# Matmul operands moved 64 bytes down against the weight slots in SBUF, and fp32 products of constants put ahead of the 512-column units, in a three-block transformer kernel

## The chip, the cores and the metric

The program runs on one core of one Trainium2 chip. The metric is the device time of one execution in microseconds, lower is better; the time quoted is the median of the runs of a kernel. The profile is of one execution, taken by the hardware profiler.

## What is computed

256 tokens of width 1024 pass through a chain of blocks, all in fp32. First come two layers of a block with modulation, for a latent sequence x and a context sequence ctx of 256 tokens each:

```
for layer in range(2):
    h  = h  + 0.5 * g1  * swiglu(prenorm(h),  ffn1)      # both sequences: 512 tokens
    hc = hc + 0.5 * cg1 * swiglu(prenorm(hc), ffn1)
    mix_l, mix_c = (even_mixer, odd_mixer)[layer](prenorm(h), prenorm(hc))
    h  = h + gm * (mix_l @ mix_w_out)                     # the context too in layer 0
    h  = h + 0.5 * g2 * swiglu(prenorm(h), ffn2)          # the context too in layer 0
return rmsnorm(h)
swiglu(h) = (silu(h @ w_g) * (h @ w_u)) @ w_out           # 1024 -> 2816 -> 1024
```

The even mixer is a Fourier mix with gated linear attention, the odd one a short convolution with differential attention. Behind them, for the 256 tokens of x alone, come a retention block, a feed-forward block c0, a dilated attention block, and a feed-forward block c1, each with a residual and a layer norm. The weights, some 400 MB, are read once.

## The kernel before

**Products.** Each fp32 product is made of three fp32r products (`product3`, L271): weights and activations are split into a high and a low part, and hi x hi, hi x lo and lo x hi are summed in PSUM. The split weights lie in three slots of 8192 bytes per partition each (`w_hi`, `w_lo`), written by ScalarE (line L105 in the profile) and VectorE (L109) from four slots `w_raw` that SyncE's queue loads. In the profile all these products are "L98 PE MATMUL bank<-x_hi,w_hi" and its like. Normally a 128x128 block of the weights is the stationary operand and the activations x, hid, even, odd, rt or at move past it: 512 columns wide in the stages of both sequences, 256 in the stages of one. In some projections the roles are exchanged (`project_rows`, L316): the activations are stationary and 256 columns of weights move ("bank<-w_hi,x_hi"). Below, a wide product is one of 512 columns, a narrow one is one of 256.

**Order.** The order of all engines is the program's. A feed-forward stage (`pe_ffn`, L832; called a0, b0, a1, b1, c0, c1) goes over its 22 blocks of 128 hidden columns two at a time: j = 0, 2, ... 10, then the products with w_out for these (4 chunks of two units), then j = 12 ... 20, then w_out again. One j is two units of 48 products. After each j, and after each chunk of w_out, `between` may put in a few fp32 products for the modulation: four-row-group products with the tile `sums`, or with `fold`. a0, b0 and a1 have 512 columns, b1, c0 and c1 have 256.

**Places.** All tiles have fixed places. `hT`, `ident`, `ones`, `cs`, `diag` and other small tiles come first, then `w_raw`, `w_hi`, `w_lo`, then coef (64 bytes), rs (96), lam (32) and a pad of 64 bytes, then a work area in which `place` puts the activations at XN, MID or TEMPS. XN and MID are multiples of 256 bytes, and the slots are multiples of 8192, so in the kernel before the work area begins at the weights' position modulo 256. Three constants shift single tiles: the narrow input x2 is placed at XN + BACK, BACK = -64; the hidden tile of the narrow stages (`hidden`, L819), and the tiles of the odd mixer and of retention, at MID + FORTH, FORTH = 192, which is -64 modulo 256. The wide x, the wide hidden tile, the tile even_hi and even_lo, and the tiles of the dilated attention but for at_hi have no shift.

**The extra product.** `pe_realign` (L648) issues one fp32 product of 256 columns of constants into a spare PSUM bank that nobody reads. It is called ahead of j = 4 in b1, c0 and c1 (`if j == 4 and n == T`), ahead of the output product of retention, and once in the dilated attention.

Of the kernel before, what the change touches and what calls it, by code (L numbers as in the profile page):

```python
# [7 lines left out]
P = 128  # L8
F32 = mybir.dt.float32
F32R = mybir.dt.float32r  # L10
# [5 lines left out]
KC = D // P  # L16
T = 256
# [32 lines left out]


XN, MID, TEMPS, WORK = 0, 32768, 90496, 106880
PAD, BACK, FORTH = 64, -64, 192
UNIT = 2048
NRAW, NSPLIT = 4, 3

# [267 lines left out]
def pe_pair(e, u, x, n, names, taken):  # L324

    for q in range(2):
        bank = e.bank(names[q], *taken[q])
        project(e, u, q * P, x, n, bank).then_inc(e.k.product, names[q])
    u.last = names[1]
# [315 lines left out]
        e.matmul(bank[:, 0:P], k.ident[:, :], k.ones[:, :], True, True)  # L645


def pe_realign(e):  # L648

    k = e.k  # L650
    bank = e.bank("spare", None, None)
    del e.used[k.bank_at["spare"]]
    for _ in range(1):
        e.matmul(bank[:, 0:T], k.ident[:, :], k.small_t[:, 0:T], True, True)


def pe_rms_rows(e, nid, n, taken):
# [166 lines left out]
def in_name(f, j, base, q):  # L824
    return (f, "in", j, base, q)


def out_name(f, half, m):
    return (f, "out", half, m)


def pe_ffn(e, f, w_in, w_out, x, n, between, gate):  # L832
    k, e.ada_owed = e.k, True
    for half, (j0, jn) in enumerate(HALVES):
        for j in range(j0, j0 + jn, 2):
            names = [in_name(f, j, base, q) for base in range(2) for q in range(2)]
            taken = [(k.scalar, (f, "silu", j, q)) for q in range(2)] + [(k.vector, (f, "gated", j, q)) for q in range(2)]
            if j == 0 and f == "a0":
                pass
            elif j == 0:  # L840
                us = [take(e, (f, "in", j, base), w_in, 0, KC, base * FFN, 256) for base in range(2)]
                project_first(e, us, x, n, names, taken)
            else:
                if j == 4 and n == T:
                    pe_realign(e)
                for base in range(2):
                    u = take(e, (f, "in", j, base), w_in, 0, KC, base * FFN + j * P, 256)
                    pe_pair(e, u, x, n, names[2 * base:2 * base + 2], taken[2 * base:2 * base + 2])
            between(e)
        if half == 0:  # L850
            gate(e)
        hid, hk = hidden(k, (f, half), n), jn // 2
        for c in range(KC // 2):
            names = [out_name(f, half, 2 * c + q) for q in range(2)]
            banks = [e.bank(names[q], k.vector, ("h", f, half, 2 * c + q)) for q in range(2)]
            for part in range(2):
                u = take(e, (f, "out", half, c, part), w_out, j0 + part * hk, hk, c * 256, 256)
                for q in range(2):
                    project(e, u, q * P, hid, n, banks[q], range(part * hk, part * hk + hk), part * hk, part == 0,
                            part == 1).then_inc(k.product, (names[q], part))  # L860
                u.last = (names[1], part)
            between(e)
# [872 lines left out]
class Odd:  # L1735
    NS = 3

    def __init__(self, k):
        at = MID + FORTH
        self.q = k.place("df_q", at, [P, 6, T])  # L1740
        self.k = k.place("df_k", at + 6144, [P, 6, 2 * T])
        self.v = k.place("df_v", at + 18432, [P, 4, 768])
        self.z3 = k.place("df_z", at + 8192, [P, 3, 2, T])
        self.cs = k.place("df_cs", at + 36864, [P, 2, T])
        self.rot = k.place("df_rot", at + 38912, [P, P])
        self.raw = k.place("df_raw", at + 39424, [P, 4, T])
        self.rt = k.place("df_rt", at + 43520, [P, 2, T])
        self.y = k.place("df_y", at + 45568, [P, 2, T])

        self.sc = k.place("df_sc", at + 47616, [P, 12, 8])  # L1750

        self.norm = k.place("df_norm", at + 48000, [P, 3, 12])
        self.sq = k.place("df_sq", at + 48192, [P, P])
        self.e = k.place("df_e", TEMPS, [P, self.NS, 2, 2 * T])

        self.aT = k.place("df_aT", at + 30720, [P, self.NS, 4, P])
        self.o = k.place("df_o", at + 39424, [P, 12, P])

        self.out = Operand(("mix", 1), k.place("odd_hi", at + FORTH + 48704, [P, KC, T], F32R), k.place("odd_lo", at, [P, KC, T], F32R))

        self.dst = [self.q[:, m, :] for m in range(6)] + [self.k[:, m, 0:T] for m in range(6)]

# [1340 lines left out]
def build(nc, io):  # L3103
    with ExitStack() as ctx:
        def sb(name, shape, dt=F32):
            return ctx.enter_context(nc.sbuf_tensor(name, shape, dt))

        def sem(name):
            return ctx.enter_context(nc.semaphore(name))

        k = Kernel()
        k.nc, k.io, k.new_sem = nc, io, sem
        k.hT, k.small_t, k.ident = sb("hT", [P, KC, 2 * T]), sb("small", [P, SMALL_N]), sb("ident", [P, P])
        k.ones, k.eps, k.one = sb("ones", [P, P]), sb("eps", [P, 2]), sb("one", [P, 1])
        k.cs, k.fold, k.mod_t = sb("cs", [P, KC, 38]), sb("fold", [P, 8]), sb("mod", [P, 2 * MODS * KC, 2])
        k.sel = sb("sel", [P, 39])
        k.mean = k.cs[:, :, :].rearrange("p k c -> p (k c)")[:, 0:P]
        k.gate, k.rs2, k.diag = sb("gate", [P, KC, 2]), sb("rs2", [P, 24]), sb("diag", [P, 4, P])
        k.raw = sb("w_raw", [P, NRAW, UNIT])
        k.whi, k.wlo = sb("w_hi", [P, NSPLIT, UNIT], F32R), sb("w_lo", [P, NSPLIT, UNIT], F32R)  # L3120
        k.coef, k.rs, k.lam = sb("coef", [P, KC, 2]), sb("rs", [P, 24]), sb("lam", [P, 8])
        sb("pad", [P, PAD // 4])
        k.work = (nc.sbuf_base + 31) // 32 * 32
        assert k.work + WORK <= nc.sbuf_top
        k.placed = {}
        k.psum = [ctx.enter_context(nc.psum_tensor(f"bank{i}", [P, 512], F32)) for i in range(8)]
        k.acc = k.place("acc", TEMPS, [P, 2 * T])
        k.spread = k.acc[:, T:2 * T]
        k.sq = k.place("sq", TEMPS + 2048, [P, 2, 2 * T])
        k.mean_row = k.sq[:, 0, T:2 * T]  # L3130
        k.tmp = k.place("tmp", TEMPS + 6144, [P, 2, 2 * T])
        k.sg = k.sq2 = k.place("sg", TEMPS + 10240, [P, 2, 2 * T])
        k.ada_rows = k.place("ada_rows", TEMPS + 14336, [P, 2, 256])
        k.sums = [k.place(f"sums{i}", MID + 49152 + 4096 * i, [P, 2, 512]) for i in range(2)]
        k.x2 = Operand(None, k.place("x2_hi", XN + BACK, [P, KC, T], F32R), k.place("x2_lo", XN + BACK + 8192, [P, KC, T], F32R))
        k.x = Operand(None, k.place("x_hi", XN, [P, KC, 2 * T], F32R), k.place("x_lo", XN + 16384, [P, KC, 2 * T], F32R))

        k.product = Signal("product", sem("s_product"))
        k.scalar, k.w_hi = Signal("scalar", sem("s_scalar")), Signal("w_hi", sem("s_w_hi"))
        k.vector, k.w_lo = Signal("vector", sem("s_vector")), Signal("w_lo", sem("s_w_lo"))  # L3140
        k.pooled = Signal("pooled", sem("s_pooled"))
        k.raw_in = [Signal(f"raw{i}", sem(f"s_raw{i}"), 16) for i in range(NRAW)]
        k.bias_in = [Signal(f"bias{i}", sem(f"s_bias{i}"), 16) for i in range(4)]
        k.loads, k.bank_at = {}, {}
        k.stream, k.split, k.units, k.others = [], [], {}, []
        counting = [True]

        def after(ahead, others):

            if counting[0]:  # L3150
                k.others.append((len(k.stream) + ahead, others))
        k.after = after

        for program in (pe_program, act_program, dve_program, pool_program, sp_program):
            program(Engine(k))
        counting[0] = False
        for signal in (k.product, k.scalar, k.w_hi, k.vector, k.w_lo, k.pooled, *k.raw_in, *k.bias_in, *k.loads.values()):
            signal.value = 0

        block = ctx.enter_context(nc.Block())  # L3160

        @block.sync
        def _(e):
            sp_program(Engine(k, e))

        @block.tensor
        def _(e):
            pe_program(Engine(k, e))

        @block.scalar  # L3170
        def _(e):
            act_program(Engine(k, e))

        @block.vector
        def _(e):
            dve_program(Engine(k, e))

        @block.gpsimd
        def _(e):
            pool_program(Engine(k, e))  # L3180
# [125 lines left out]
```

How the kernel before makes its waits and increments, by code:

```python
    def then_inc(self, signal, *events):  # L69
        signal.value += signal.step
# [18 lines left out]
    def wait_ge(self, signal, event):  # L89
        if self.eng is None:
            return
        n = signal.at[event]
        if n > self.waited.get(signal.name, 0):
            self.eng.wait_ge(signal.sem, n)
            self.waited[signal.name] = n
# [41 lines left out]
    def bank(self, name, signal, event, hold=False, of=None):  # L137
        if of is not None:
            b = of[self.turns.get(of, 0) % len(of)]
            self.turns[of] = self.turns.get(of, 0) + 1
        else:
            while self.turn in self.holds:
                self.turn = (self.turn + 1) % 8
            b = self.turn
            self.turn = (b + 1) % 8
        if hold:
            self.holds.add(b)
        if b in self.used:
            self.wait_ge(*self.used[b])
        self.used[b] = (signal, event)
        self.k.bank_at[name] = b
        return self.k.psum[b]
# [45 lines left out]
def take(e, name, w, k0, kn, c0, cn, split=True, book=False, summed=False):  # L201
# [11 lines left out]
            u.turn = len(k.split)  # L213
            u.hi_flat, u.lo_flat = k.whi[:, u.turn % NSPLIT, 0:kn * cn], k.wlo[:, u.turn % NSPLIT, 0:kn * cn]
            u.hi, u.lo = (t.rearrange("p (k c) -> p k c", k=kn) for t in (u.hi_flat, u.lo_flat))
            k.split.append(u)
        k.stream.append(u)
        k.units[name] = u
    u = k.units[name]
    if book:
        return u
    if split:
        e.wait_ge(k.w_hi, u.index)
        e.wait_ge(k.w_lo, u.index)
    else:
        e.wait_ge(k.raw_in[u.slot], u.index)
```

## Time and profile before

| | |
|---|---|
| time, median of 3 runs | 2644.91 us (2644.59 to 2647.29) |
| time of the profiled execution | 2645.05 us |
| span from first to last instruction | 2643.3 us |
| mean granted TensorE clock | 0.993 of full speed |
| TensorE busy | 2583.0 us of the span (98%) |
| VectorE busy | 1483.6 us (56%) |
| ScalarE busy | 1040.9 us (39%) |

An instruction's duration in the profile runs from its issue to its modelled end, and matmuls overlap in it: two consecutive products of 389 ns can start 227 ns apart. The rate at which TensorE works is therefore read from the starts, or from a piece of the chain of waits: its length divided by the number of matmuls in it. An fp32 product appears as two MATMUL records.

### The profile page before, as it was taken

To read this page: it belongs to the slowest core of one execution; us is meant where nothing else is said; L and a number is where in the kernel's file an instruction comes from. 1 tells how busy PE (TensorE), PEld (TensorE's weight loads), DVE (VectorE), ACT (ScalarE), POOL (GpSimd) and SP (SyncE) were. 2 spreads that over 40 slices of the span, in tenths; PEclk is the share of its full clock that TensorE was granted. 3 is DMA by queue.
4 is the path that set the end of the run, shared out by engine and by line. 5 is a ranking of instruction groups with operands and counts; after the bars stand their busy time and mean duration, and the time that the engine had idled before them with its cause. 6 is when DMAs were issued, how large, how long until landed. Compare 5 with 4: busy or idle time off the path is not lost.

```text
span 2643.3 us, 40453 instructions
## 1 busy us (share of the span) xinstructions
PE 2583.0 (98%) x17454; PEld 2278.0 (86%) x17454; DVE 1483.6 (56%) x1985; ACT 1040.9 (39%) x1402; POOL 199.2 (8%) x192
## 2 busy tenths in 40 slices
PE   6999999999999999999999999999999999999998
PEld 4788888877888888888878899999999999988998
DVE  5666654746556546553345565566555554565655
ACT  3322223534222224222233554453754454554544
POOL 0000000211000000000011000010020020144001
PEclk9999999999999999999999999999999999999999
DMA  7544455214444444443153165565446566763462
GB/s 259 177 159 149 154 166 164 64 62 149 133 149 146 141 159 152 146 156 120 60 171 126 49 195 188 182 211 169 146 152 196 182 194 187 218 148 119 149 207 91
DMA packets 376080, 405.98 MB, mean 154 GB/s; under 512 B 7264, under 2 KB 352176, under 8 KB 375904
## 3 DMA queue, kind: packets, MB, share of 16 engines
q1 hardware_dynamic: 375904, 403.40, 47.9%
q8 instruction: 138, 2.26, 0.4%
q14 instruction: 38, 0.31, 0.0%
HBM read 402.25 MB, written 1.12 MB: 153 GB/s over the span
## 4 chain that ended last, share of the span: by engine, by line
PE 90%; DVE 4%; issue 3%; ACT 2%; POOL 1%; DMA 1%; SPq 0%; DVEq 0%; POOLq 0%; ACTq 0%
PE bank L98 89%; DVE w_lo L109 1%; PE bank L101 1%; ACT w_hi L105 1%; POOL acc L109 1%; DVE tmp L117 0%; DMA ident<-in_ident 0%; DVE df_sc L126 0%; ACT df_e L106 0%; ACT x_hi L105 0%; DVE hT L117 0%; DMA w_raw<-in_ada_w 0%; ACT at_pT L105 0%; ACT at_e L106 0%; ACT L105 0%
## 5 line engine op out<-in xcount | busy, mean ns | idle before, releaser
L109 DVE TENSOR_TENSOR w_lo<-w_raw,w_hi 128x2048 fp32r<-128x2048 f32 (+2 forms) x331 | 698.4, 2114 | 740.4 <-ACT w_hi L105 739.8
L98 PE MATMUL bank<-x_hi,w_hi 128*128 128x256 f32 (+1 forms) x3000 | 976.8, 326 | 5.0 <-DVE w_lo L109 2.0
L98 PE MATMUL bank<-x_hi,w_lo 128*128 128x256 f32 (+1 forms) x3000 | 966.5, 322 | 0.0
L98 PE MATMUL bank<-x_lo,w_hi 128*128 128x256 f32 (+1 forms) x3000 | 961.6, 322 | 0.0
L105 ACT ACTIVATE w_hi<-w_raw 128x2048 fp32r<-128x2048 f32 (+2 forms) x331 | 578.9, 1753 | 377.3 <-PE bank L98 221.2
L98 PEld LDWEIGHTS bank<-x_hi,w_hi 128*128 128x128 f32 x3000 | 564.7, 188 | 66.0 <-issue 15.1
L98 PEld LDWEIGHTS bank<-x_hi,w_lo 128*128 128x128 f32 x3000 | 564.7, 188 | 47.6
L98 PEld LDWEIGHTS bank<-x_lo,w_hi 128*128 128x128 f32 x3000 | 562.3, 188 | 47.3 <-issue 0.7
L98 PE MATMUL bank<-hid_hi,w_hi 128*128 128x512 f32 (+1 forms) x1056 | 353.0, 334 | 0.0
L98 PE MATMUL bank<-hid_hi,w_lo 128*128 128x512 f32 (+1 forms) x1056 | 351.4, 333 | 0.0
L98 PE MATMUL bank<-hid_lo,w_hi 128*128 128x512 f32 (+1 forms) x1056 | 351.2, 333 | 0.0
L105 ACT ACTIVATE hid_hi<-tmp 128x512 fp32r<-128x512 f32 (+1 forms) x132 | 69.3, 525 | 415.5 <-DVE tmp L109 415.5
L98 PEld LDWEIGHTS bank<-hid_hi,w_hi 128*128 128x128 f32 x1056 | 198.2, 188 | 24.6 <-issue 4.1
L98 PEld LDWEIGHTS bank<-hid_hi,w_lo 128*128 128x128 f32 x1056 | 198.2, 188 | 20.8
L98 PEld LDWEIGHTS bank<-hid_lo,w_hi 128*128 128x128 f32 x1056 | 198.3, 188 | 20.2
L117 DVE SCALAR_TENSOR_TENSOR sums<-w_raw,cs,sums 128x512 f32<-128x512 f32 x308 | 207.7, 746 | 0.0
L109 POOL TENSOR_TENSOR acc<-acc,sq 128x256 f32<-128x256 f32 (+1 forms) x60 | 60.9, 1015 | 1475.1 <-ACT sq L105 1474.0
L98 PE MATMUL bank<-w_hi,x_hi 128*128 128x256 f32 x544 | 156.7, 288 | 0.0
L98 PE MATMUL bank<-w_lo,x_hi 128*128 128x256 f32 x544 | 152.7, 281 | 0.0
L98 PE MATMUL bank<-w_hi,x_lo 128*128 128x256 f32 x544 | 152.6, 281 | 0.0
L105 ACT ACTIVATE sg<-bank 128x512 f32<-128x512 f32 (+1 forms) x132 | 63.5, 485 | 214.3 <-PE bank L98 214.3
L109 DVE TENSOR_TENSOR hid_lo<-tmp,hid_hi 128x512 fp32r<-128x512 f32 (+1 forms) x132 | 73.8, 559 | 78.0 <-ACT hid_hi L105 78.0
(278 smaller groups left out, 2333.5 us busy)
## 6 DMA issues: line engine op xcount, KB each, us to landing
w_raw<-in_ffn_w_in SPq DMA_DIRECT2D x88, 1024.0 KB, 6.1
w_raw<-in_ada_w SPq DMA_DIRECT2D x72, 1024.0 KB, 8.0
w_raw<-in_ffn_w_up SPq DMA_DIRECT2D x44, 1024.0 KB, 5.2
w_raw<-in_attn_w_in SPq DMA_DIRECT2D x36, 1024.0 KB, 5.2
w_raw<-in_ffn_w_out SPq DMA_DIRECT2D x32, 768.0 KB, 4.7
w_raw<-in_ret_w_in SPq DMA_DIRECT2D x24, 1024.0 KB, 5.4
w_raw<-in_ffn_w_out SPq DMA_DIRECT2D x32, 640.0 KB, 4.3
w_raw<-in_odd_w_in SPq DMA_DIRECT2D x12, 1024.0 KB, 5.4
```

What stands on the lines that cost most here:

```text
L98: return Issued(self.eng and self.eng.matmul(out, lhsT, rhs, start=start, stop=stop, skip_group_check=loose))
L101: return Issued(self.eng and self.eng.transpose(out, in_, self.k.ident[:, :]))
L105: return Issued(self.eng and self.eng.activation(out, in_, func, bias=bias, scale=scale))
L109: return Issued(self.eng and self.eng.tensor_tensor(out, a, b, op))
L117: return Issued(self.eng and self.eng.scalar_tensor_tensor(out, a, s, b, op0, op1))
```

## The change

It has three parts.

1. coef, rs and lam, 192 bytes together, move from behind the weight slots to ahead of them, and the pad behind the slots grows from 64 to 192 bytes. The work area now begins 192 bytes, that is -64 modulo 256, after the weights' position. BACK and FORTH become 0, so x2, the narrow hidden tile and the tiles of the odd mixer and of retention keep their -64 against the weights; at_hi too. The wide x, the wide hidden tile, even_hi and even_lo, the wide and narrow use of x in both mixers, and at_lo go from 0 to -64.
2. `pe_realign` takes a number of 128-column blocks and a number of repeats; the moving operand is now the identity tile, repeated, where it was the tile small.
3. In a0 and b0 it is called ahead of each j from 4 to 20, with the lengths of the table REALIGN, and in a1 once, ahead of j = 4, with 4 blocks. The calls in the narrow stages keep their place and length.

```diff
-PAD, BACK, FORTH = 64, -64, 192
+PAD, BACK, FORTH = 64, 0, 0
...
-def pe_realign(e):
+REALIGN = {4: (2, 1), 6: (1, 1), 8: (4, 1), 10: (2, 2), 12: (1, 2), 14: (4, 2), 16: (2, 3), 18: (1, 3), 20: (2, 1)}
+
+
+def pe_realign(e, blocks=2, times=1):
 
     k = e.k
     bank = e.bank("spare", None, None)
     del e.used[k.bank_at["spare"]]
-    for _ in range(1):
-        e.matmul(bank[:, 0:T], k.ident[:, :], k.small_t[:, 0:T], True, True)
+    wide = k.ident[:, :].rearrange("p (o n) -> p o n", o=1).broadcast_to([P, blocks, P])
+    for _ in range(times):
+        e.matmul(bank[:, 0:blocks * P].rearrange("p (o n) -> p o n", o=blocks), k.ident[:, :], wide, True, True)
...
-                if j == 4 and n == T:
+                if n == T and j == 4:
                     pe_realign(e)
+                if n == 2 * T and f != "a1" and j in REALIGN:
+                    pe_realign(e, *REALIGN[j])
+                if f == "a1" and j == 4:
+                    pe_realign(e, 4, 1)
...
-        self.out = Operand(("mix", 1), k.place("odd_hi", at + FORTH + 48704, [P, KC, T], F32R), k.place("odd_lo", at, [P, KC, T], F32R))
+        self.out = Operand(("mix", 1), k.place("odd_hi", at + 48640 + 256, [P, KC, T], F32R), k.place("odd_lo", at, [P, KC, T], F32R))
...
+        k.coef, k.rs, k.lam = sb("coef", [P, KC, 2]), sb("rs", [P, 24]), sb("lam", [P, 8])
         k.raw = sb("w_raw", [P, NRAW, UNIT])
         k.whi, k.wlo = sb("w_hi", [P, NSPLIT, UNIT], F32R), sb("w_lo", [P, NSPLIT, UNIT], F32R)
-        k.coef, k.rs, k.lam = sb("coef", [P, KC, 2]), sb("rs", [P, 24]), sb("lam", [P, 8])
-        sb("pad", [P, PAD // 4])
+        sb("pad", [P, 3 * PAD // 4])
```

## Rows read from the trace of the kernel before

**Rows 1.** The page: busy time, share and instructions; granted clock in 40 slices.

```profile
PE 2583.0 (98%) x17454; PEld 2278.0 (86%) x17454; DVE 1483.6 (56%) x1985; ACT 1040.9 (39%) x1402; POOL 199.2 (8%) x192
PEclk9999999999999999999999999999999999999999
```

**Rows 2.** The chain that ended last: shares of the span by engine.

```profile
PE 90%; DVE 4%; issue 3%; ACT 2%; POOL 1%; DMA 1%; SPq 0%; DVEq 0%; POOLq 0%; ACTq 0%
```

**Rows 3.** Waits of PE: total us, times, longest.

```profile
PE bank L98 <- DVE w_lo L109: 3.0, 4, 1.0
```

**Rows 4.** Busy time by stretch, all engines: a0, then b0.

```profile
60.00:450.00 390.00, 389.12 (x1819) 314.55 (x1819) 237.66 (x321) 109.30 (x120) 8.48 (x7) 1.00 0.49 161
620.00:1010.00 390.00, 390.00 (x1875) 316.14 (x1878) 219.43 (x299) 108.80 (x120) 9.95 (x8) 1.00 0.45 150
```

**Rows 5.** Groups of PE by form, whole span: count, busy us, mean ns, idle before.

```profile
L98 PE MATMUL bank<-x_hi,w_hi 128*128 128x256 f32 x1792 | 501.4, 280 | 3.6 <-DVE w_lo L109 2.0 <-DVE x_lo L117 1.1 <-ACT x_hi L105 0.2
...
L98 PE MATMUL bank<-x_hi,w_hi 128*128 128x512 f32 x1208 | 475.4, 394 | 1.4 <-ACT sg L105 0.8 <-DVE x_lo L117 0.5
...
L98 PE MATMUL bank<-hid_hi,w_hi 128*128 128x512 f32 x528 | 207.3, 393 | 0.0
...
L98 PE MATMUL bank<-even_hi,w_hi 128*128 128x512 f32 x64 | 25.4, 397 | 2.9 <-ACT even_hi L105 2.9
```

**Rows 6.** Chain pieces: start us, length us, what; wide products of a0, then a1.

```profile
109.89 16.32 PE bank L98 x72
...
1214.91 155.27 PE bank L98 x685
```

**Rows 7.** Chain pieces: narrow products on x, not shifted (even mixer), then shifted (b1).

```profile
456.92 10.08 PE bank L98 x84
...
1599.99 140.08 PE bank L98 x1236
...
1576.00 4.59 PE bank L98 x39
```

**Rows 8.** Timeline of PE around the call of pe_realign in b1: start, us.

```profile
1586.56 0.28 PE L98 MATMUL bank<-x_lo,w_hi 128*128 128x256 f32 x1
1586.68 0.28 PE L98 MATMUL bank<-x_hi,w_lo 128*128 128x256 f32 x1
1586.80 0.59 PE L98 MATMUL bank<-small,ident 128*128 128x256 f32 x2
1587.04 0.47 PE L98 MATMUL bank<-x_hi,w_hi 128*128 128x256 f32 x1
1587.35 0.28 PE L98 MATMUL bank<-x_lo,w_hi 128*128 128x256 f32 x1
1587.47 0.28 PE L98 MATMUL bank<-x_hi,w_lo 128*128 128x256 f32 x1
1587.59 0.28 PE L98 MATMUL bank<-x_hi,w_hi 128*128 128x256 f32 x1
```

**Rows 9.** Timeline of PE: other fp32 products ahead of shifted narrow ones.

```profile
1574.80 0.51 PE L98 MATMUL bank<-fold,ada_rows 128*128 128x8 f32 x4
1575.16 0.36 PE L98 MATMUL bank<-x_hi,w_hi 128*128 128x256 f32 x1
1575.36 0.28 PE L98 MATMUL bank<-x_lo,w_hi 128*128 128x256 f32 x1
1575.48 0.28 PE L98 MATMUL bank<-x_hi,w_lo 128*128 128x256 f32 x1
1575.60 0.28 PE L98 MATMUL bank<-x_hi,w_hi 128*128 128x256 f32 x1
1575.72 0.28 PE L98 MATMUL bank<-x_lo,w_hi 128*128 128x256 f32 x1
...
1841.74 2.73 PE L98 MATMUL bank<-rt_v,rt_S 128*128 128x512 f32 x6
1843.91 0.68 PE L98 MATMUL bank<-w_hi,x_hi 128*128 128x256 f32 x1
1844.43 0.28 PE L98 MATMUL bank<-w_lo,x_hi 128*128 128x256 f32 x1
```

**Rows 10.** Timeline of PE after `sums` in a0: start, us.

```profile
105.16 0.64 PE L98 MATMUL bank<-sums,sel 128*32 128x256 f32 x8
105.73 0.50 PE L98 MATMUL bank<-x_hi,w_hi 128*128 128x512 f32 x1
106.07 0.39 PE L98 MATMUL bank<-x_lo,w_hi 128*128 128x512 f32 x1
106.30 0.39 PE L98 MATMUL bank<-x_hi,w_lo 128*128 128x512 f32 x1
106.53 0.40 PE L98 MATMUL bank<-x_hi,w_hi 128*128 128x512 f32 x1
106.77 0.39 PE L98 MATMUL bank<-x_lo,w_hi 128*128 128x512 f32 x1
107.00 0.40 PE L98 MATMUL bank<-x_hi,w_lo 128*128 128x512 f32 x1
107.23 0.39 PE L98 MATMUL bank<-x_hi,w_hi 128*128 128x512 f32 x1
107.46 0.39 PE L98 MATMUL bank<-x_lo,w_hi 128*128 128x512 f32 x1
107.69 0.39 PE L98 MATMUL bank<-x_hi,w_lo 128*128 128x512 f32 x1
```

**Rows 11.** Groups of PE by form: even mixer (440 to 545 us), odd mixer (1375 to 1556 us).

```profile
L98 PE MATMUL bank<-w_hi,x_hi 128*128 128x256 f32 x128 | 36.5, 285 | 0.0
...
L98 PE MATMUL bank<-w_hi,x_hi 128*128 128x256 f32 x96 | 28.8, 300 | 0.0
L98 PE MATMUL bank<-x_hi,w_hi 128*128 128x256 f32 x96 | 28.0, 293 | 1.3 <-DVE x_lo L117 1.1
```

## The prediction

> **What bounds the kernel.** Read the page first: TensorE is busy 98% of the span at full clock, VectorE 56% [rows 1]. The chain of waits says the same: 90% of it is TensorE's own work [rows 2]. The waits of PE for split weights come to 3.0 us in all [rows 3]. By stretch, a0 and b0 keep PE busy without a gap, with VectorE at 61% and 56% of the time and the DMA engines under half [rows 4]. So nothing is late behind TensorE in the wide stages, and each nanosecond taken from a matmul there, or added to it, is a nanosecond of the time.
>
> Next, how fast the matmuls follow each other. There are 1208 + 528 + 64 = 1800 wide products, each of three matmuls: 5400 [rows 5]. In steady work they start 16.32 / 72 = 226.7 ns apart in a0 and 155.27 / 685 = 226.7 ns apart in a1 [rows 6]. 512 columns at the granted 2.4 GHz are 213.3 ns, so each carries 13.3 ns, or 32 cycles, of something else.
>
> The narrow ones tell what part of it depends on place. 256 columns are 106.7 ns. With x at the weights' position modulo 256 (even mixer) they start 10.08 / 84 = 120.0 ns apart: again 13.3 ns over. With operands at -64 (b1) they do so at 140.08 / 1236 = 113.3 ns, 6.7 over, and in the same stage a little earlier at 4.59 / 39 = 117.7, 11 over [rows 7]. So at -64 there are two steady rates, and one is kept until something breaks the stream. The call of pe_realign leads from the slow to the fast one: 0.12 us between starts before it, 0.11 after [rows 8]. Other fp32 products ahead of narrow ones end differently: after `fold` the starts lie 0.12 us apart, after a 512-column product 0.11 [rows 9].
>
> **The move, wide products.** No row shows a wide fp32r product at -64. The bounds: nothing gained, 226.7; or all of the 13.3 ns gone, 213.3, which would be 5400 x 13.3 = 72 us. I take the narrow rows as the model, because the excess at 0 is the same 13.3 ns for both widths. That speaks for a cost paid once per matmul, where its stream and the load of the next block meet, and not one per column. Then a wide product at -64 costs 220.0 in the good state, saving 6.7 ns, or 224.4 (213.3 + 11) in the poor one, saving 2.2.
>
> Which state? The narrow stages settle once and run on for over a thousand matmuls. a0 and b0 are cut again and again by `sums` and `fold`: after `sums` eight starts at 0 lie 0.23 to 0.24 us apart before the stream settles [rows 10]. At -64 each such break draws a state anew. `fold` gave the poor one in the narrow case, the extra product of 256 columns and one of 512 the good one [rows 8, 9]. I take three quarters good, one quarter poor: 0.75 x 6.7 + 0.25 x 2.2 = 5.6 ns, and 5400 x 5.6 = 30.0 us. All good gives 36.0, all poor 11.9.
>
> **The move, narrow products.** 3 x 128 in the even mixer and 3 x (96 + 96) in the odd one go from 0 to -64 [rows 11]: 960 matmuls, cut often by other products, half in each state: 960 x 4.4 = 4.2 us; between 2.1 and 6.4. at_lo joins at_hi at -64 (192 matmuls, under 1 us), taken as nothing. The fp32 products of the mixers get other places too; bounded by the same 6.7 ns on a few hundred, and of unknown sign, they are left at nothing.
>
> A rule stands against all this. The Trainium skill, page "SBUF — State Buffer", section "Who interferes with whom", says that PE waits for no one and that its two read ports, for the moving operand and for the weight load, are independent. By it a place would not matter; this trace disagrees, with 120.0 against 113.3 ns for the same matmul. The Trainium skill's page "TensorE: Matmul & The Clock Gate", section "Back-to-back issue gap", gives N/2.4 + 2.5 ns, 215.8 at 512 columns; by it the wide part would save 5400 x 10.9 = 59 us, an estimate; the narrow rows do not come down to its 109.2 ns here.
>
> **The extra products.** Without the call in b1, the next matmul on x_hi,w_hi would have started at 1586.80 and the one three places on 0.35 us later; the latter started at 1587.59, 0.79 us later: 0.44 us for 256 columns [rows 8]. Three 512-column products: the second matmul behind them starts 2.69 us after their start, and 0.11 of it is that matmul's own distance, which leaves 0.86 us each [rows 9]. So the cost goes by columns. The table has 2 + 1 + 4 + 4 + 2 + 8 + 6 + 3 + 2 = 32 blocks of 128, 16 times the 256-column product: 16 x 0.44 = 7.04 us, in each of a0 and b0, and 0.88 in a1: 15.0 us in all. Nothing covers it, since PE waits for nothing there [rows 4]; nearly all of them stand where `sums` or `fold` has broken the stream already, so no second settling is added. The spare bank turns the order of banks by one, but in these stages seven or eight banks serve five allocations per j of 22 us, so the next user finds its bank read long ago.
>
> VectorE and ScalarE see their tiles moved against each other by multiples of 64 bytes; taken as nothing, and hidden by PE in any case [rows 4]. Where PE gets 2.5% faster VectorE goes from 61% to 63% of a0.
>
> **The sum.** 2645.05 - 30.0 - 4.2 + 15.0 = 2625.8 us. The profiled execution lies 0.1 us above the median of 2644.91, so 2625.7.
>
> **The rivals.**
>
> *A. The wide products do go faster, in both states mixed (the forecast).* From 11.9 + 2.1 saved up to 36.0 + 6.4 saved; with at least half in the good state (5400 x 4.4 = 24.0) it is 2614 to 2637. Chance 0.53.
>
> *B. The wide ones find only the poor state.* The 128-column and odd lengths of the table are untried before fp32r products at -64. 2645.0 - 11.9 - 2.1 + 15.0 = 2646.0. Chance 0.10.
>
> *C. The wide ones don't change (the move does nothing).* Weight loads are busy for 81% of a0 [rows 4], so a wide product leaves them slack, and its excess may come from elsewhere, with the equal 13.3 ns a chance. Then 2645.0 - 4.2 + 15.0 = 2655.8, slower than before. It decides from the point where the mean saving of a wide matmul is under (15.0 - 4.2) / 5400 = 2.0 ns. Against it: equal excess at both widths. Chance 0.17. If the place does nothing for the narrow ones either, 2645.0 + 15.0 = 2660.0; the three narrow rates of this trace speak against it [rows 7]: 0.04. This last case is the one that the Trainium skill's SBUF page stands for.
>
> *D. The narrow stages lose their good state.* pe_realign reads the identity for both operands now. If that ends in the poor state, some 1390 matmuls of each of b1, c0 and c1 (all behind j = 2) go from 113.3 to 117.7: 3 x 1390 x 4.4 = 18.4 us, and the time would be 2625.7 + 18.4 = 2644.1. Against it: the same length and the same stationary tile. Chance 0.09.
>
> *E. The wide ones get slower.* After `sums` six starts take 107.46 - 106.07 = 1.39 us, 231.7 ns each [rows 10]; if -64 made that lasting, 5400 x 5.0 = 27 us more: 2645.0 + 27 - 4.2 + 15.0 = 2682.8. Chance 0.07.
>
> **Numbers.** What a measurement can tell from no change is 0.2%, 5.3 us: 2639.6 to 2650.2. Faster: A, and a part of D: 0.57. Same: most of B and half of D: 0.12. Slower: C, E and the rest: 0.31. The range goes from 2614 (all wide and narrow products in the good state give 2645.0 - 36.0 - 6.4 + 15.0 = 2617.6, and 3 us for fp32 products that gain too) to 2660, which takes in B, C and D and leaves E; A alone is 2614 to 2637.
>
> **What would show it.** In the profile after, a piece of the chain inside a0 or a1, its length over its count: 220 in the good state, 224.4 in the poor, 226.7 if C holds. The mean duration of the wide groups, 389 to 394 ns now [rows 5], follows by the same difference. The stretch of a1 with no `sums` behind 1215 us shows one state alone. In b1, c0 and c1 the starts after the extra product should stay at 113.3; else it is D. The products of ident with ident should take about 0.21 us per 128 columns. The forecast is wrong if the wide stream has a steady state of its own that the narrow one doesn't have: its weight load has slack, the narrow one's has little.

## The result, and the profile after

The changed kernel takes 2693.49 us (median of 4 runs, 2689.58 to 2694.50) against 2644.76 for the kernel before, 48.7 us or 1.8% more. The comparison on record puts the ratio at 1.0165, with a 95% interval of 1.0142 to 1.0187; it is not the quotient of the two medians, but both lie well clear of no change. The ratios further down are of the same kind. I had forecast 2625.7, faster, in a range that ended at 2660. The change loses 49 us where I expected it to gain 19.

The page of the changed kernel, the lines that answer to [rows 1] and [rows 2]:

```profile
PE 2630.3 (98%) x17520; PEld 2290.0 (85%) x17520; DVE 1483.1 (55%) x1985; ACT 1041.2 (39%) x1402; POOL 199.9 (7%) x192
PEclk9999999999999999999999999999999999999999
...
PE 89%; DVE 4%; issue 3%; ACT 3%; DMA 1%; POOL 1%; SPq 0%; DVEq 0%; POOLq 0%; ACTq 0%
```

TensorE is still all of it, at the same clock, and busy 47 us longer. VectorE and ScalarE do what they did. 66 MATMUL records are new: 33 fp32 products of two records each, 16 in a0, 16 in b0 and 1 in a1.

Groups of PE by form, whole span, for [rows 5] (count, busy us, mean ns, idle before):

```profile
L98 PE MATMUL bank<-x_hi,w_hi 128*128 128x256 f32 x1792 | 503.5, 281 | 3.9 <-DVE w_lo L109 2.0 <-DVE x_lo L117 1.1 <-ACT x_hi L105 0.3
...
L98 PE MATMUL bank<-x_hi,w_hi 128*128 128x512 f32 x1208 | 485.1, 402 | 1.1 <-ACT sg L105 0.6 <-DVE x_lo L117 0.5
...
L98 PE MATMUL bank<-hid_hi,w_hi 128*128 128x512 f32 x528 | 210.5, 399 | 0.0
```

The narrow group is as it was, 281 ns for 280. The wide ones went from 394 to 402 and from 393 to 399 (the groups of x and of hid). Pieces of the chain of waits give the distance of the starts, for [rows 6] and [rows 7]: wide in a1, narrow in the even mixer, narrow in b1. In the even mixer it is the weights that move and x that is stationary.

```profile
1261.91 103.13 PE bank L98 x442
...
475.45 9.66 PE bank L98 x82
...
1644.93 135.09 PE bank L98 x1192
```

103.13 / 442 = 233.3 ns for the wide product, where it was 226.7. 9.66 / 82 = 117.8 in the even mixer, where it was 120.0. 135.09 / 1192 = 113.3 in b1, as before. So a wide matmul pays 20.0 ns beyond its 213.3, three times the 6.7 ns of the good narrow state, and neither the 6.7 nor the 11 of the forecast. The timeline of PE around an added product in a1 (for [rows 8] and [rows 10]):

```profile
1093.40 0.39 PE L98 MATMUL bank<-x_hi,w_lo 128*128 128x512 f32 x1
1093.63 1.02 PE L98 MATMUL bank<-ident 128*128 128x512 f32 x2
1094.09 0.79 PE L98 MATMUL bank<-x_hi,w_hi 128*128 128x512 f32 x1
1094.72 0.39 PE L98 MATMUL bank<-x_lo,w_hi 128*128 128x512 f32 x1
1094.95 0.40 PE L98 MATMUL bank<-x_hi,w_lo 128*128 128x512 f32 x1
1095.19 0.39 PE L98 MATMUL bank<-x_hi,w_hi 128*128 128x512 f32 x1
1095.42 0.40 PE L98 MATMUL bank<-x_lo,w_hi 128*128 128x512 f32 x1
1095.65 0.39 PE L98 MATMUL bank<-x_hi,w_lo 128*128 128x512 f32 x1
```

Behind it the starts lie 0.23 to 0.24 us apart, as they do without it.

Where the time went, from the starts of the first product of each stage in each profile (us; the last four columns are experiments of the next section):

```
                       before  after  move_only  products_only  wide_plus64  no_products
a0 (from its first)     379.8  397.3    388.9        389.9         384.8        381.7
even mixer              226.8  228.5    228.4        226.8         226.4        226.5
b0                      368.2  385.1    378.1        375.2         371.4        368.2
norm ahead of a1          6.9    8.5      6.9          6.9           6.9          6.9
a1                      364.0  375.0    374.1        364.9         367.3        364.0
odd mixer               189.2  186.6    187.6        187.7         189.1        189.9
b1                      187.3  187.7    187.3        187.1         187.1        194.1
retention               210.5  210.0    210.2        210.5         210.8        210.2
c0                      190.2  189.7    189.5        189.3         189.3        195.7
dilated, projections    136.3  140.9    138.5        141.1         136.1        138.4
dilated, the rest       159.5  158.9    159.1        158.2         158.8        159.0
c1                      195.7  195.7    196.2        202.4         196.0        201.5
```

45.4 of the 49.4 us of span are in a0, b0 and a1. The other large line is the dilated attention's projections, 4.6 us.

Differences of a microsecond or two in this table need the granted clock beside them. The first 8 us from 28 us on, of the kernel before, products_only and no_products (the clock is the third number from the end):

```profile
28.00:36.00 8.00, 8.00 (x53) 5.33 (x46) 3.51 (x11) 1.72 (x5) 0.00 (x0) 0.86 1.09 348
```

```profile
28.00:36.00 8.00, 8.00 (x47) 4.73 (x40) 2.49 (x9) 1.29 (x3) 0.00 (x0) 0.68 1.09 348
```

```profile
28.00:36.00 8.00, 6.99 (x36) 3.99 (x29) 2.55 (x6) 1.70 (x5) 0.00 (x0) 0.57 1.09 348
```

TensorE stands at 1.2 GHz for part of these 8 us, in some executions for longer. A share of 0.68 for 0.86 takes 0.18 of 8 us of full speed away, 1.4 us; 0.57 takes 2.3 us. The 1.6 us of the norm ahead of a1 are of the same kind, since the granted clock there was 0.80 in the changed kernel and 1.00 in the kernel before. In b0 and a1 the clock was full in the kernel before, in products_only and in the changed kernel.

### The profile page after: what moved, and what is told of

The parts are those of the page before. It is cut to its first block, busy times and chain, and to the rows that moved or that the text cites. A ratio compares the mean times of both kernels' runs of the same rounds, so it can differ in the third digit from the quotient of the medians.

```text
span 2692.7 us, 40582 instructions
## 1 busy us (share of the span) xinstructions
PE 2630.3 (98%) x17520; PEld 2290.0 (85%) x17520; DVE 1483.1 (55%) x1985; ACT 1041.2 (39%) x1402; POOL 199.9 (7%) x192
## 4 chain that ended last, share of the span: by engine, by line
PE 89%; DVE 4%; issue 3%; ACT 3%; DMA 1%; POOL 1%; SPq 0%; DVEq 0%; POOLq 0%; ACTq 0%
PE bank L98 88%; DVE w_lo L109 1%; ACT w_hi L105 1%; PE bank L101 1%; POOL acc L109 1%; DMA w_raw<-in_ada_w 0%; DVE hT L117 0%; DVE tmp L117 0%; DVE df_sc L126 0%; DMA ident<-in_ident 0%; DVE sums L117 0%; ACT df_e L106 0%; ACT x_hi L105 0%; ACT at_pT L105 0%; ACT at_e L106 0%
## 5 line engine op out<-in xcount | busy, mean ns | idle before, releaser
L98 PE MATMUL bank<-x_hi,w_hi 128*128 128x256 f32 (+1 forms) x3000 | 988.5, 330 | 5.0 <-DVE w_lo L109 2.0
```

The source lines that it names most:

```text
L98: return Issued(self.eng and self.eng.matmul(out, lhsT, rhs, start=start, stop=stop, skip_group_check=loose))
```

## The experiments

**Apart: the move alone, the products alone.** The first leaves the calls in the wide stages out of the changed kernel (everything else as there):

```diff
-                if n == 2 * T and f != "a1" and j in REALIGN:
-                    pe_realign(e, *REALIGN[j])
-                if f == "a1" and j == 4:
-                    pe_realign(e, 4, 1)
```

> The changed kernel without the products ahead of the wide units (they stay in the narrow stages). Theory 1, a wide matmul at -64 starts every 233.3 ns whatever stands ahead of it: 5400 x 6.67 = 36.0 us more, 4 less in the mixers, some 5 more in the dilated attention: about 2679 to 2683, and every long wide stretch of the chain at 233.3 ns. Theory 2, the added products themselves put the wide stream into a slow state: wide stretches at 220 or 226.7 ns and 2618 to 2645.

The second is the kernel before with the new `pe_realign` (its body is that of the change) and its calls, and nothing moved:

```diff
...
-                if j == 4 and n == T:
+                if n == T and j == 4:
                     pe_realign(e)
+                if n == 2 * T and f != "a1" and j in REALIGN:
+                    pe_realign(e, *REALIGN[j])
+                if f == "a1" and j == 4:
+                    pe_realign(e, 4, 1)
```

> The kernel before with the added products and nothing moved. Theory 1: the wide stretches stay at 226.7 ns and the time rises by the products alone, 15.0 us: 2660. Theory 2, that the products slow the wide stream: wide stretches over 226.7 ns and up to 2695. If the products ahead of j find cover: under 2652.

move_only takes 2676.41 us, 1.0114 times the kernel before (1.0092 to 1.0136). products_only takes 2668.50, 1.0078 times (1.0053 to 1.0102). The first is 3 us under the range of its first theory, the second 8 us over its 2660: in the stage table c1 is 6.7 us longer and the dilated projections are 4.8 us longer, two narrow stages that no added product of the wide ones touches. A wide piece of the chain in a1, of move_only and then of products_only:

```profile
1244.99 95.20 PE bank L98 x408
```

```profile
1235.82 94.29 PE bank L98 x416
```

95.20 / 408 = 233.3 ns with the move and no added product; 94.29 / 416 = 226.7 with the products and no move. So the wide rate follows the place, and the products do nothing to it at either place. Theory 1 holds in both. In the stage table the move costs 9.1, 9.9 and 10.1 us in a0, b0 and a1, near the 1584 x 6.67 = 10.6 of each stage, and the products cost 10.1, 7.0 and 0.9.

The 7.0 and 0.9 are the forecast's terms to the tenth. In a0 there are 3 us more, and about half of them is a wait that I had ruled out. The timeline of PE in the changed kernel's a0:

```profile
270.43 0.64 PE L98 MATMUL bank<-sums,sel 128*32 128x256 f32 x8
272.42 1.99 PE L98 MATMUL bank<-ident 128*128 128x512 f32 x4 [1.35 <-ACT ada_rows L105]
273.84 0.82 PE L98 MATMUL bank<-x_hi,w_hi 128*128 128x512 f32 x1
```

The spare bank fell on the one that `sums` had just filled and ScalarE had yet to read. `pe_sums` holds that bank only until its own products are issued, not until they are read, so the next allocation may get it. In products_only the same wait is 1.67 us:

```profile
268.94 1.98 PE L98 MATMUL bank<-ident 128*128 128x512 f32 x4 [1.67 <-ACT ada_rows L105]
```

The rest is the clock at the start of a0, shown above: 7.0 + 1.7 + 1.4 = 10.1 us. In the changed kernel, where the clock of those 8 us was 0.85, nearly that of the kernel before, a0 adds up without it: 9.1 for the move, 7.0 for the products and 1.35 of waiting make the 17.5 measured. In no_products, whose a0 has the same instructions as the kernel before, the clock alone gives 1.9 us more.

**A list of places.** A kernel of its own runs 72 fp32r matmuls of the kernel's pattern (hi x hi, hi x lo, lo x hi, with blocks changing) for each place of the moving operand against the stationary one. It computes nothing of the reference.

```diff
+SECTIONS = [(n, p, 0, 128) for n in (512, 256) for p in (*range(0, 256, 32), 16, 48, 208, 240)]
+SECTIONS += [(n, p, s, 128) for n in (512, 256) for p, s in ((64, 64), (0, 64), (128, 128), (64, 128), (0, 128))]
+SECTIONS += [(512, p, 0, m) for m in (64, 32) for p in (0, 192)]
...
+            for n, p, s, m in SECTIONS:
+                e.matmul(psum[7][:, 0:T], ident[:, :], hT[:, 0, 0:T], start=True, stop=True)
...
+                        e.matmul(bank[0:m, 0:n], hi, x0, start=kk == 0, stop=False)
+                        e.matmul(bank[0:m, 0:n], lo, x0, start=False, stop=False)
+                        e.matmul(bank[0:m, 0:n], hi, x1, start=False, stop=kk == KC - 1)
```

> Not the computation: 72 fp32r matmuls for each of a list of places, with the moving operand 0 to 240 bytes above the stationary one modulo 256, 512 and 256 columns wide, some with the stationary operand moved as well, some with a stationary block of 64 or 32 columns. Theory 1, the excess depends on the place of one operand against the other: 226.7 ns at 0 and 233.3 at 192 for 512 columns, 120.0 and 113.3 (or 117.7) for 256, the same at (64, 64) and (128, 128) as at (0, 0), and less excess with a narrower stationary block. Some other place may give 220 or less for 512 columns. Theory 2, the excess depends on the absolute place: (64, 64) differs from (0, 0). Theory 3, it comes from something else in the kernel, such as the other engines' accesses: all places alike here.

Mean distance of the starts behind the 20th, in ns:

```
bytes of the moving operand against the stationary one, modulo 256
            0      16     32     48     64     96     128    160    192    208    224    240
512 wide  226.7  231.6  233.3  233.3  228.9  233.3  232.6  234.3  233.4  234.7  233.3  236.6
256 wide  120.0  118.7  116.7  118.4  117.8  119.9  118.6  118.7  113.3  119.1  118.4  117.1
both operands up by 64: 226.7 and 120.0; by 128: 226.7 and 120.0
only the stationary one up by 64 (that is 192): 233.4 and 113.3
the stationary one up by 128, the moving one by 64 (192 again): 233.4 and 117.8
512 wide, stationary block of 64 columns: 229.8 at 0, 232.7 at 192; of 32: 231.7 and 231.6
```

This gives the kernel's rates again in a program with no other engine at work: 226.7 and 120.0 at 0, 233.4 and 113.3 at 192, which is -64. For the wide stream it is the place of one operand against the other that counts: the two entries at 0 with both moved, and the two further ones at 192, give the same as before. The narrow one has 113.3 and 117.8 at 192, the two steady rates of [rows 7]. In the mixers' exchanged projections the weights move, so x at -64 is place 64 of this list, with its 117.8: the 117.8 of the even mixer. The two widths don't follow each other. The best wide place is the narrow stream's worst of these, and from 160 to 240, where the narrow one is no worse than 119.1, the wide one pays 233.3 to 236.6. My forecast had them parallel. A narrower block doesn't take the excess away: with 32 columns it is 18 ns at both places tried.

**Finer, and one thing changed at a time.**

```diff
+SECTIONS = [(512, p, 0, 128) for p in (0, 4, 8, 12, 20, 24, 236, 244, 248, 252, 196, 188)]
...
+SECTIONS += [(512, k, 0, 128) for k in ("line", "column", "xlo192", "xlo64", "wlo64", "wlo192", "fp32")]
+SECTIONS += [(n, p, 0, 128) for n in (384, 128) for p in (0, 192)]
+SECTIONS += [(256, k, 0, 128) for k in ("line", "column", "xlo0", "wlo64")]
...
+                        if p == "column":
+                            x0, x1 = (xs[home][:, a:a + 1].broadcast_to([P, n]) for a in (at0, at1))
```

> Not the computation: again 72 fp32r matmuls for each of a list of cases. Finer places around 0 for 512 columns and around 192 for 256. Theory 1, that the two streams meet in lines of 64 bytes: 4 to 12 bytes beside the good place give nearly the same rate, within 3 ns. Theory 2, the good places are sharp: already 4 bytes beside them it is 230 ns and more, 117 and more. Then one thing changed each: the moving operand 16 columns read again and again (line) or one column (column), the low activations or low weights at another place, plain fp32, 384 and 128 columns. If the excess is made where the moving stream crosses SBUF, line and column take it away (216 ns or less for 512 columns); if it is made behind the array, they leave it at 227. Plain fp32 should show about 216 ns between records, as the product of constants does in the kernel before.

At 4 bytes off the best place the wide rate is 237.1 ns, at 8 it is 233.3, at 12 it is 228.9: Theory 1, lines of 64 bytes, falls. With the low activations, or the low weights, alone moved off 0 it is 228.9 to 232.2. "line" (the same 16 columns again and again) gave 242.0, so a short stretch is no better. "column" (one column, 512 times) gave 217.8, which leaves 4.4 ns of the 13.3. The groups of PE in the stretch of "column" (L106 to L108 are the three matmuls):

```profile
L106 PE MATMUL bank<-x_p,w_hi 128*128 128x512 f32 x18 | 6.9, 382 | 0.0
L108 PE MATMUL bank<-x_p,w_hi 128*128 128x512 f32 x18 | 6.8, 378 | 0.0
L107 PE MATMUL bank<-x_p,w_lo 128*128 128x512 f32 x17 | 6.5, 381 | 0.0
```

Their 378 to 382 ns stand against 389 for the ordinary operand at 0. So what the moving operand reads has a part in the excess; more is not shown, since "line" went the other way and a narrow stream at 192 gained only 1.5 ns by reading one column (111.8 for 113.3). Plain fp32 was a miss: I expected some 216 ns between records and got 429.2, since the 216 of the kernel before belong to products of 256 columns. An fp32 product of 512 columns thus takes 858.4 ns, only 5 more than four times 213.3, where an ordinary fp32r matmul carries 13.3 or more by itself.

384 columns cost 173.3 ns at 0 and 176.7 at 192, against 160 for the columns themselves. Set beside the other widths this is the most useful pair of the list:

```
excess over the columns' own time, ns     256 wide   384 wide   512 wide
moving operand at 0                         13.3       13.3       13.3
at 192 (-64); 256 in its good state          6.7       16.7       20.0
```

At 0 the excess is one cost per matmul, whatever the width. At 192 it grows with the width, and the narrow stream's gain has turned into a loss already at 384 columns. (128 columns took 111.7 ns at both places, over twice their 53.3, and say nothing on it.)

**All 64 places.**

```diff
+SECTIONS = [(n, p, 0, 128) for n in (512, 256) for p in range(0, 256, 4)]
```

> Not the computation: 72 fp32r matmuls at every place of the moving operand in steps of 4 bytes, 0 to 252 above the stationary one, for 512 and for 256 columns. Theory 1, that places are sharp and irregular: most of the 64 wide places give 228 to 240 ns, 0 gives 226.7 and is the best or among the best few; most narrow ones give 117 to 125 and only a few 113.3. If a wide place under 225 ns exists, the wide stages of the kernel can gain by it. Theory 2, a smooth dependence: neighbours within 1 ns of each other.

The best wide place is 0, with 226.7 ns; then 60 (227.8), 28 and 108 (227.8), 64 and others (228.9). The worst are 68, 116, 132, 196 and 244 with 240.0. The first and last matmul of four stretches, at 0, 4, 64 and 192 (33, 31, 32 and 32 matmuls; start us, duration us):

```profile
32.75 0.39 PE L85 MATMUL bank<-x_p,w_lo 128*128 128x512 f32 x1
...
40.00 0.39 PE L84 MATMUL bank<-x_p,w_hi 128*128 128x512 f32 x1
...
50.82 0.40 PE L86 MATMUL bank<-x_p,w_hi 128*128 128x512 f32 x1
...
57.94 0.40 PE L86 MATMUL bank<-x_p,w_hi 128*128 128x512 f32 x1
...
306.72 0.39 PE L86 MATMUL bank<-x_p,w_hi 128*128 128x512 f32 x1
...
313.82 0.39 PE L84 MATMUL bank<-x_p,w_hi 128*128 128x512 f32 x1
...
858.74 0.40 PE L86 MATMUL bank<-x_p,w_hi 128*128 128x512 f32 x1
...
865.97 0.39 PE L84 MATMUL bank<-x_p,w_hi 128*128 128x512 f32 x1
```

7.25 / 32 = 226.6 ns, 7.12 / 30 = 237.3, 7.10 / 31 = 229.0 and 7.23 / 31 = 233.2. Narrow, 113.3 is reached at 64, 112 and 192, and 123.3 at 4 and 180. At 64 the first list had 117.8, and at 8 this one has 116.7 where the finer list had 120.0; wide, 240 has 233.3 here and 236.6 in the first list. These may be places with two steady rates, as [rows 7] showed for -64, but the operands also lie 256 bytes further apart modulo 512 in this list, and no run separates the two. The kernel before lies at the best place for its wide products, so none of these 64 places gives them anything.

**Does the list hold for the kernel?** The work area 64 bytes above the weights, the narrow tiles kept at -64, no product added:

```diff
-PAD, BACK, FORTH = 64, -64, 192
+PAD, BACK, FORTH = 128, -128, 128
...
-        self.out = Operand(("mix", 1), k.place("odd_hi", at + FORTH + 48704, [P, KC, T], F32R), k.place("odd_lo", at, [P, KC, T], F32R))
+        self.out = Operand(("mix", 1), k.place("odd_hi", at + 48896, [P, KC, T], F32R), k.place("odd_lo", at, [P, KC, T], F32R))
```

> The kernel before with the work area 64 bytes above the weights modulo 256 instead of level with them, the narrow tiles kept at -64 by BACK = -128 and FORTH = 128, no product added. If the scan of places holds for the kernel, wide matmuls start every 228.9 ns (it is 226.7 at 0 and 233.3 at -64): 5400 x 2.2 = 12 us more, less 4.5 us for the mixers' exchanged projections at 113.3 instead of 120.0 ns and 0.6 for the others: 2652. If any move off 0 costs the wide ones 6.7 ns: 2676. If -64 is bad for another reason than its place against the weights: 2640.

A wide piece in a1, and a narrow one in the even mixer:

```profile
1228.00 97.05 PE bank L98 x424
...
462.98 8.05 PE bank L98 x71
```

97.05 / 424 = 228.9 ns, the list's figure for 64, and 8.05 / 71 = 113.4 where it was 120.0; with the roles exchanged that is place 192. So the list held for the kernel at a place that it had never run at. The time is 2659.26 us, 1.0040 times the kernel before (1.0022 to 1.0059). The profiled execution spans 2653.6, 10.3 more than the profiled one before. I had expected 2652. The stage table has 11.5 us more in a0, b0 and a1, of which 2.3 is the clock at the start (0.57 there), but only 0.5 less in the mixers, where 4.5 was expected; in the odd mixer no gain is seen.

**The narrow stages.** Three kernels ask what decides their state. First, move_only with the tile small in pe_realign again:

```diff
-        e.matmul(bank[:, 0:blocks * P].rearrange("p (o n) -> p o n", o=blocks), k.ident[:, :], wide, True, True)
+        e.matmul(bank[:, 0:T], k.ident[:, :], k.small_t[:, 0:T], True, True)
```

> As move_only, but the products ahead of j = 4 in the narrow stages read the tile small again, as in the kernel before. Theory 1, what they read decides the state that the narrow stage ends in: the dilated projections come back to 113.3 ns after it and the time falls by 2 to 5 us against move_only, to 2671 to 2674. Theory 2, the state there follows from the timing of what lies ahead, whichever tile is read: 2676, within 1 us.

2679.22 us, 1.0120 times (1.0096 to 1.0145). The dilated projections took 141.0 us, where the same call with the identity had 138.5: the tile that is read is not what decides. Behind the call the stream was in the good state in move_only (identity) and in the poor one in move_small (small); in the kernel before it was good (small) and in products_only poor (identity).

Then the kernel before without any extra product:

```diff
-    for _ in range(1):
+    for _ in range(0):
```

> The kernel before with the five extra products taken out (the spare bank is still passed over). Theory 1, that the product of constants leads a narrow stream into its good state: b1, c0, c1, the output of retention and the dilated projections keep the state in which they come, several of them 117.7 ns, each such stage 5 to 7 us longer, and the time rises by 5 to 25 us. Theory 2, that any break draws the state and the product does no more than that: as many stages may come out well without it, and the time is within 10 us either way, with 2.2 us saved for the products themselves.

2657.27 us, 1.0041 times (1.0020 to 1.0063). The table above has b1, c0 and c1 at 194.1, 195.7 and 201.5 us, 6.8, 5.5 and 5.8 more. A piece in b1 and one in c1 of its profile:

```profile
1639.95 28.15 PE bank L98 x239
...
2544.91 15.19 PE bank L98 x129
```

Both are 117.8 ns. This profile is the slowest of the kernel's six executions (2667.42; the others 2652.09 to 2664.96), so its 18 us in three stages are more than the product is usually worth: the medians are 10.6 us apart, with five products of 0.44 us saved. The time lies in the range of Theory 1 and at the edge of that of Theory 2. The traces say more. In the eight profiles that have the call (all but this one) the stream behind it ran at 113.3 ns in 23 of 24 stages b1, c0 and c1, and here in none of three. In the dilated attention it did so in four of the eight. So the product leads to the good state nearly always in the feed-forward stages, and not everywhere.

Last, two kernels once more, unchanged: the kernel before, and products_only, whose c1 had been 6.7 us slower.

> The kernel before, word for word, profiled once more. If the state of a narrow stretch (113.3 or 117.7 ns) is fixed by the program, the dilated projections (1152 matmuls) and c1 show the same rates as in the first profile, 114.9 and 113.3 to 116.4 on average. If it is drawn in each execution, some stretch differs by the 4.4 ns, 5 to 7 us of the span, and the differences that the narrow stages show between the kernels here say nothing about the edits.

> The kernel of products_only once more. If the state of c1 is fixed by the program, c1 runs at 117.7 ns again and takes 202 us; if it is drawn in each execution, it has an even chance of 113.3 and 196 us.

A narrow piece of c1, of products_only and then of the same program again:

```profile
2539.91 25.20 PE bank L98 x214
```

```profile
2539.92 25.16 PE bank L98 x222
```

25.20 / 214 = 117.8 ns and 25.16 / 222 = 113.3. The same program had the other state. Its dilated projections took 141.1 us both times, and the kernel before repeated itself in every stage to 1.4 us (2640.69 us in all). An execution of the same kernel beside it, without a profile, took 2657.87, so the repeated profile doesn't show the whole spread. The state is likely in some stages and a draw in others. This also spreads the runs: 6.7 us of c1 is more than the 5.1 us between the fastest and the slowest run of products_only.

## Why the prediction was wrong

**The step that failed** is "I take the narrow rows as the model, because the excess at 0 is the same 13.3 ns for both widths." That the excess is paid once per matmul is true at place 0 (13.3 ns at 256, 384 and 512 columns) and false at -64, where it is 6.7, 16.7 and 20.0 ns. The narrow stream's gain at -64 therefore says nothing of the wide one's: the wide product starts every 233.3 ns there (move_only and the list), 20.0 over its 213.3. 5400 x 6.67 = 36.0 us are lost by that rate, where I had put 30.0 us gained; the 4752 of them in a0, b0 and a1 lost 29.1 in the stage table. One coincidence, 13.3 and 13.3 at place 0, carried the whole term. The list shows that the two widths have different good places (0 for one; 64, 112 and 192 for the other). It is the term with the wrong sign, and large enough to decide the outcome by itself.

**Rival E** named the outcome: -64 makes the wide stream slower for good. It had 0.07, and its price, 5.0 ns from the settling starts of [rows 10], was 1.7 ns short. The price came from starts that were still settling at place 0, which have nothing to do with -64, so that it came near is luck. I had excluded nothing on that side, yet ended the range at 2660, though no row bounded a wide matmul at -64 from above.

**The products.** 7.04 us for b0 and 0.88 for a1 were forecast; 7.0 and 0.9 were measured. The sentence that "the next user finds its bank read long ago" was wrong in a0: 1.35 us of idle time in one place, before the added product itself, from a bank that ScalarE had yet to empty. That they would lead the wide stream to a good state was wrong: it has one rate at each of 0 and -64, with or without them.

**The narrow products of the mixers** had 4.2 us of gain in the forecast. The even mixer's went from 120.0 to 117.8 only, since the weights move there and x at -64 is place 64; it lost 1.7 us in all, by its wide part. The odd mixer is 2.6 us shorter, but 1.5 us shorter in products_only too, where nothing was moved, so about 1 us of it is left for the change. I had treated both roles alike.

**Rival D** was half right. The dilated projections did lose the good state, 4.6 us, but b1, c0 and c1 did not in the changed kernel, and the identity as the moving operand isn't the reason (move_small had the loss with small).

**Added up:** a0, b0 and a1 give 45.4 us (29.1 in move_only, 18.0 in products_only), the dilated projections 4.6, the norm ahead of a1 and the even mixer 3.3 (1.6 of it the clock), the odd mixer -2.6, the rest -1.3: 49.4.

The rule of the Trainium skill that I set against the rows (page "SBUF — State Buffer", section "Who interferes with whom": PE has independent ports for the moving operand and the weight load, and waits for no one) does not agree with the list of places either: 226.7 to 240.0 ns for the same wide matmul by place alone. No other engine was at work there, so it is the independence of the two ports that the list speaks against. Of the page "TensorE: Matmul & The Clock Gate", section "Back-to-back issue gap", I took N/2.4 + 2.5 ns, 215.8 for 512 columns. The section gives it for a matmul by itself, and for a stream of loads and matmuls it has about 131 ns; no fp32r stream here comes down to either, and the one that reads a single column comes nearest, with 217.8.

**Open:** why 0 is the best wide place and -64 a poor one, and why the excess at -64 grows with the width. That the weight load has slack in a wide product, which the prediction named as a possible reason, was not tested by itself. A meeting of two streams in lines of 64 bytes doesn't fit, since 4 bytes beside 0 cost 10 ns. What decides between the two narrow states is open as well: in the dilated attention the same distances of the starts around the product, 0.32, 0.03 and 0.31 us, were followed by either (good in wide_plus64, poor in products_only).

## What to carry to other kernels

The rate of an fp32r stream with 128x128 blocks depended here on where its moving operand lies against its stationary one modulo 256 bytes, and each width had its own good places. Measure the place for the width, in a small kernel of its own, before moving tiles, since a list of 64 places takes under 2 ms of device time. Never carry an excess from one shape to another because the two happen to be equal at one point; where no row bounds the unknown price on the bad side, let the range go there. Ask which operand moves, too: with the roles exchanged the same two addresses are another place. Products of constants ahead of long narrow stretches paid for themselves here, 10.6 us between the medians for five products of 0.44 us; ahead of the wide ones they were pure cost. Before you read a stage difference of one or two microseconds, compare the granted clock of the two stretches.

## What was not expected of the hardware

- The place is sharp to the element: wide 226.7 ns at 0, 237.1 at 4 bytes, 228.9 at 12, 240.0 at 68.
- A stationary block of 32 columns has more excess (231.7 ns) than one of 128 at the best place (226.7), though its load takes 109 ns for 189.
- The excess over the columns' time is 13.3 ns at 0 for 256, 384 and 512 columns, and 6.7, 16.7 and 20.0 ns at -64.
- An fp32 product of 512 columns took 858.4 ns, 5 over four times 213.3.
- Reading the same 16 columns 32 times is slower (242.0 ns) than reading 512 columns, and reading one column 512 times faster (217.8).
- Two runs of one program can differ by 6.7 us because one stage of 1584 matmuls settled at 117.8 instead of 113.3 ns.
